# Differential attention: scores moved between the first four and the last two transpositions of a step

## The chip, the cores and the metric

One core of a Trainium2 chip runs the whole program. The metric is device time in microseconds (us), the median of several executions. The kernel before takes 3136.89 us (three runs, 3135.58 to 3138.68).

## What is computed

The program is a two-layer block (LRU, convolution, forgetting attention, gated feed-forward) followed by two hybrid layers. The change touches one part of each hybrid layer, differential attention over 512 latent tokens (and, in the first hybrid layer, 256 context tokens). For each of four heads there are two sets of scores, and the output uses the difference of their softmaxes:

```python
def diff_attn_dense(q, k, v, lam):
    s = jnp.einsum('bqhcd,bkhcd->bhcqk', q, k).astype(jnp.float32) * (q.shape[-1] ** -0.5)
    p = jax.nn.softmax(s, axis=-1)
    a = (p[:, :, 0] - lam * p[:, :, 1]).astype(v.dtype)
    return jnp.einsum('bhqk,bkhv->bqhv', a, v)
```

The result is normalised per head (`diff_head_norm`) and multiplied by a gate.

## The kernel before

The program is one instruction list per engine, written by hand: TensorE (PE), VectorE (DVE), ScalarE (ACT), GpSimd (POOL) and SyncE (SP). Each engine takes its own list strictly in the order written, and semaphores hold it where another engine's result is needed.

Differential attention is a list of jobs, one for a head and 128 query tokens: in hybrid layer 0 five jobs for each head (four latent ones with 768 keys, then one context job that covers all 256 context queries with 256 keys), 20 in all; in hybrid layer 1 four latent jobs for each head, 16 in all. One job n passes through these pieces:

- **scores** (PE, L970; matmuls L986, for context L977): two sets, into PSUM banks 0 to 2 for even n and 3 to 5 for odd n. It waits until the exponentials of job n-2 have freed these banks.
- **maxima** (DVE, L2393, instruction L2398): negative row maxima of both sets, straight from PSUM.
- **exps** (ACT, L1674, instruction L1680): two exponentials of 768 elements (four of 256 for a context job), with their sums; the last frees the score banks.
- **probs** (DVE, L2401; L2407, L2410, L2416): reciprocals, and the difference of the two sets. It waits for the freed banks.
- **transposes** (PE, L992): four 128x128 transpositions into bank 6 (L1001), which wait for probs; then, for a latent job, two more into the first half of bank 7 (L1006). Bank 7 is also where values writes its result, so these two wait for evac of job n-1.
- **evac on ACT** (L1685): copies bank 6 (L1689) and then bank 7 (L1693) to the buffer DAT.
- **values** (PE, L1009, L1020): six matmuls of 128 columns with V (four for a context job), into bank 7. It waits for both copies by ACT.
- **evac on DVE** (L2419, L2424): scales the result out of bank 7. **squares** (ACT, L1695) sums its squares.
- After the last latent job and after the context job of a head: **scale** (DVE, L2433), **turn** (PE, L1024, L1029), which transposes the scaled head back through bank 6, and **post** (DVE, L2438).

The order of the work is that of the step loops. In step n, PE issues scores(n+2), values(n-1), transposes(n) and, where job n-2 ended a head, turn(n-2). ACT issues exps(n+1), evac(n), squares(n-1). DVE issues probs(n), post(n-3), maxima(n+2), evac(n-1), scale(n-2). After the last job PE goes on with the first products of the next stage, `pe_head` (L579, matmuls L594 to L596).

Of the kernel before, what the change touches and what calls it, by code (L numbers as in the profile page):

```python
# [249 lines left out]
def build(nc, x, ctx_in, w8, wb, wm, wf_in, wg_in, params, rows, lru_w, sgu_w, sgu_b, rope, rot, nbias, vlat, mrow, wrow,  # L250
# [9 lines left out]
    def sem(name):  # L260
        if name not in sems:
            sems[name] = cx.enter_context(nc.semaphore(name))
        return sems[name]
# [154 lines left out]
    DE, DAT0, DSQ = cv(2, 2 * TA), cv(TA), cv(P)  # L418
    assert cv.at <= hyb_at + 2 * KT * SLAB
    DAT = [DAT0, RST[:, 0:TA]]  # L420
# [52 lines left out]
    def past(name, layer):  # L473

        return in_layer0[name] if layer else 0
# [26 lines left out]
    def wait(eng, s, v):  # L502

        if not (isinstance(v, int) and v <= 0):
            eng.wait_ge(s, v)
# [460 lines left out]
    def pe_da(pe, st):  # L966
        ly, jobs = st.layer, st.jobs
        nj = len(jobs)

        def scores(j):  # L970
            n, h, p = j["n"], j["h"], 3 * (j["n"] % 2)
            wait_free(pe, st, p, n // 2)
            lo, hi = slice(0, 64), slice(64, 128)
            if j["ctx"]:
                for qb in range(2):
                    for c, r in ((0, lo), (1, hi)):
                        mm = pe.matmul(PS[:, p + c, qb * TC:(qb + 1) * TC], Q[r, h, T + qb * P:T + (qb + 1) * P],  # L977
                                       K[r, h, T:TA], start=True, stop=True, skip_group_check=True)
            else:
                q0 = P * j["qb"]  # L980
                half = sem("da_half")
                for i, (r, b, c0, k0, k1) in enumerate(((lo, p + 1, 0, T, TA), (hi, p + 2, 0, TC, TA),
                                                        (lo, p, 0, 0, T), (hi, p + 1, TC, 0, TC))):
                    if i == 3:
                        pe.wait_ge(half, past("da_half", ly) + sum(not k["ctx"] for k in jobs[:n]) + 1)
                    mm = pe.matmul(PS[:, b, c0:c0 + k1 - k0], Q[r, h, q0:q0 + P], K[r, h, k0:k1], start=True,  # L986
                                   stop=True, skip_group_check=True)
                    if i == 0:
                        mm.then_inc(half, 1)
            mm.then_inc(full[p], 1)  # L990

        def transposes(j):  # L992
            n = j["n"]
            pe.wait_ge(sem("da_probs"), past("da_probs", ly) + n + 1)
            wait_free(pe, st, 6, n)
            outs = sum(i["last"] for i in jobs[:max(n - 2, 0)])
            wait(pe, sem("da_y"), past("da_y", ly) + outs)
            e = DE[:, n % 2, :]
            for i in range(4):
                o = i if not j["ctx"] else 2 * (i % 2) + i // 2  # L1000
                mm = pe.transpose(PS[:, 6, o * P:(o + 1) * P], e[:, i * P:(i + 1) * P], IDENT[:, :])  # L1001
            mm.then_inc(full[6], 1)
            wait(pe, sem("da_evac"), past("da_evac", ly) + n)
            if not j["ctx"]:
                for i in range(4, 6):
                    mm = pe.transpose(PS[:, 7, (i - 4) * P:(i - 3) * P], e[:, i * P:(i + 1) * P], IDENT[:, :])  # L1006
                mm.then_inc(full[7], 1)

        def values(j):  # L1009
            n, h = j["n"], j["h"]  # L1010
            nl = sum(not i["ctx"] for i in jobs[:n + 1])
            pe.wait_ge(freed[6], st["free", 6] + n + 1)
            pe.wait_ge(freed[7], st["free", 7] + nl)
            wait(pe, sem("da_evac"), past("da_evac", ly) + n)
            at = DAT[n % 2]
            for qb in range(1 + j["ctx"]):
                tiles = (4, 5) if j["ctx"] else range(6)
                for i, t in enumerate(tiles):
                    o = i * TC + qb * P if j["ctx"] else i * P
                    mm = pe.matmul(PS[:, 7, qb * P:(qb + 1) * P], at[:, o:o + P], V[:, t, h * P:(h + 1) * P],  # L1020
                                   start=i == 0, stop=i == len(tiles) - 1, skip_group_check=True)
            mm.then_inc(sem("da_o"), 1)

        def turn(j):  # L1024

            pe.wait_ge(sem("da_scaled"), past("da_scaled", ly) + j["g"] + 1)
            pe.wait_ge(freed[6], st["free", 6] + min(j["n"] + 3, nj))
            for i in range(2 if j["ctx"] else 4):
                mm = pe.transpose(PS[:, 6, i * P:(i + 1) * P], DO[:, j["g"] % 2, i * P:(i + 1) * P], IDENT[:, :])  # L1029
            mm.then_inc(sem("da_turned"), 1)  # L1030

        pe.wait_ge(sem("rope_done"), past("rope_done", ly) + 8)
        for b in range(8):
            wait_free(pe, st, b, 0)
        scores(jobs[0])
        scores(jobs[1])
        for n in range(nj + 2):
            if n + 2 < nj:
                scores(jobs[n + 2])
            if 0 <= n - 1 < nj:  # L1040
                values(jobs[n - 1])
            if n < nj:
                transposes(jobs[n])
            else:
                pe_head(pe, st.merge, n - nj)
            if 0 <= n - 2 < nj and jobs[n - 2]["last"]:
                turn(jobs[n - 2])
        if st.merge.ctx:
            pe_head(pe, st.merge, 2)
# [620 lines left out]
    def act_da(act, own, st):  # L1670
        ly, jobs = st.layer, st.jobs
        nj = len(jobs)

        def exps(j):  # L1674
            n, p = j["n"], 3 * (j["n"] % 2)
            act.wait_ge(sem("da_max"), past("da_max", ly) + n + 1)
            k, w = (4, TC) if j["ctx"] else (2, TA)
            src = PS[:, p:p + 3, :].rearrange("p a b -> p (a b)")
            for i in range(k):
                ins = act.activation(DE[:, n % 2, i * w:(i + 1) * w], src[:, i * w:(i + 1) * w], ACT.Exp,  # L1680
                                     bias=SMALL[:, 4 * (n % 2) + i:4 * (n % 2) + i + 1],
                                     accum_out=SMALL[:, 16 + 4 * (n % 4) + i:17 + 4 * (n % 4) + i])
            ins.then_inc(freed[p], 1)

        def evac(j):  # L1685
            n = j["n"]
            at = DAT[n % 2]
            act.wait_ge(full[6], st["full", 6] + n + 1)
            act.activation(at[:, 0:T], PS[:, 6, :], ACT.Copy).then_inc(freed[6], 1)  # L1689
            if not j["ctx"]:  # L1690
                nl = sum(not i["ctx"] for i in jobs[:n])
                act.wait_ge(full[7], st["full", 7] + nl + 1)
                act.activation(at[:, T:TA], PS[:, 7, 0:TC], ACT.Copy).then_inc(freed[7], 1)  # L1693

        def squares(j):  # L1695
            n, g = j["n"], j["g"]
            act.wait_ge(sem("da_evac"), past("da_evac", ly) + n + 1)
            for i in range(2) if j["ctx"] else (j["qb"],):
                c = 40 + 4 * (g % 2) + i
                own.wait()  # L1700
                own.mark(act.activation(DSQ[:, :], DO[:, g % 2, i * P:(i + 1) * P], ACT.Square,
                                        accum_out=SMALL[:, c:c + 1]))
            if j["last"]:
                k = 2 if j["ctx"] else 4
                ss, rs = (SMALL[:, c + 4 * (g % 2):c + 4 * (g % 2) + k] for c in (40, 48))
                own.wait()
                own.link(act.activation(rs, ss, ACT.Ln, bias=EPSC[:, 0:1], scale=1.0 / P))
                act.activation(rs, rs, ACT.Exp, scale=-0.5).then_inc(sem("da_rs"), 1)

        act.preload_act_table_set("natural_log_exp_and_others")  # L1710
        for part in range(2):
            act_head(act, st.merge, part)
        exps(jobs[0])
        for n in range(nj + 1):
            if n + 1 < nj:
                exps(jobs[n + 1])
            if n < nj:
                evac(jobs[n])
            if 0 <= n - 1 < nj:
                squares(jobs[n - 1])  # L1720

# [663 lines left out]
    def dve_da(dve, own, st):  # L2385
# [60 lines left out]
        for n in range(nj + 3):  # L2446
            if n < nj:
                probs(jobs[n])
            if 0 <= n - 3 < nj and jobs[n - 3]["last"]:
                post(jobs[n - 3])  # L2450
            if n + 2 < nj:
                maxima(jobs[n + 2])
            if 0 <= n - 1 < nj:
                evac(jobs[n - 1])
            if 0 <= n - 2 < nj and jobs[n - 2]["last"]:
                scale(jobs[n - 2])

# [689 lines left out]
```

## Time and profile before

| | |
|---|---|
| median of three runs | 3136.89 us |
| the profiled execution's own time | 3136.75 us |
| its span in the profile | 3135.0 us |
| PE busy | 96% of the span |
| DVE, ACT busy | 47%, 37% |
| differential attention, hybrid layer 0 (first transposition to the first product of the next stage) | 79.07 us |
| the same, hybrid layer 1 | 65.49 us |

A busy PE is not PE at its peak, since the ends of matmuls are modelled. What one piece costs is therefore read as the distance from its start to the start of the next piece on the same engine. An engine's idle time before an instruction stands in square brackets, with what ended it.

### The profile page before, as it was taken

What the parts mean: (1) busy time and instruction counts of PE and PEld (TensorE: products, weight loads), DVE (VectorE), ACT (ScalarE), POOL (GpSimd) and SP (SyncE); (2) the same over time, 40 slices, a digit from 0 to 9 for tenths busy, and PEclk for the clock granted to TensorE, in tenths of its full rate; (3) what the DMA queues carried; (4) which work ended last, traced back from release to release, by engine and by line L of the source; (5) the groups of instructions that cost most, each with busy time, mean ns of one, the idle gap of its engine ahead of it and who ended that gap; (6) DMA issues with size and microseconds to landing.
All of it is one profiled execution on the core that took longest, in us unless ns stands there. A gap on an engine that the chain in (4) does not pass through costs nothing.

```text
span 3135.0 us, 38597 instructions
## 1 busy us (share of the span) xinstructions
PE 3008.1 (96%) x15614; PEld 2446.7 (78%) x15614; DVE 1479.8 (47%) x1976; ACT 1155.7 (37%) x1828; POOL 148.9 (5%) x206
## 2 busy tenths in 40 slices
PE   7999999999999998989999899999999999999998
PEld 5777888777778887867888788868877778878776
DVE  4645454545454556176252532163444635352344
ACT  4335233425352444145243431163222534241342
POOL 1000000110000000000000400100000000200100
PEclk9999999999999999999999999999999999999999
DMA  4242232331322221110111311211111022221322
GB/s 176 94 148 104 111 108 100 125 125 50 121 94 94 95 96 57 68 34 28 50 55 61 91 65 52 96 58 48 53 68 67 14 77 75 101 95 54 115 71 81
DMA packets 44460, 256.81 MB, mean 82 GB/s; under 512 B 6344, under 2 KB 6352, under 8 KB 20512
## 3 DMA queue, kind: packets, MB, share of 16 engines
q1 hardware_dynamic: 30528, 204.30, 18.3%
q0 software_dynamic: 13792, 50.51, 4.9%
q8 instruction: 104, 1.70, 0.2%
q14 instruction: 36, 0.29, 0.0%
HBM read 250.51 MB, written 4.28 MB: 81 GB/s over the span
## 4 chain that ended last, share of the span: by engine, by line
PE 86%; DVE 8%; ACT 3%; DMA 2%; issue 1%; POOL 1%; DVEq 0%; SPq 0%; ACTq 0%; POOLq 0%
PE PS L805 13%; PE PS L806 13%; PE PS L807 13%; PE PS L786 7%; PE PS L785 7%; PE PS L787 7%; PE PS L751 2%; PE PS L750 2%; PE PS L749 2%; DVE SMALL L2398 2%; PE PS L986 1%; DMA W<-in_w 1%; PE PS L1100 1%; PE PS L1084 1%; PE PS L1074 1%
## 5 line engine op out<-in xcount | busy, mean ns | idle before, releaser
L805 PE MATMUL PS<-HHX,WHX 128*128 128x512 f32 (+1 forms) x1456 | 510.5, 351 | 8.7 <-DVE WLX L2248 6.4
L806 PE MATMUL PS<-HL,WHX 128*128 128x512 f32 (+1 forms) x1456 | 511.5, 351 | 0.0
L1565 ACT ACTIVATE WHX<-W 128x2048 fp32r<-128x2048 f32 (+1 forms) x102 | 174.6, 1712 | 578.6 <-DMA W<-in_w 390.5
L807 PE MATMUL PS<-HHX,WLX 128*128 128x512 f32 (+1 forms) x1024 | 356.5, 348 | 0.0
L2248 DVE TENSOR_TENSOR WLX<-W,WHX 128x2048 fp32r<-128x2048 f32 x60 | 137.5, 2292 | 381.8 <-ACT WHX L1565 381.8
L805 PEld LDWEIGHTS PS<-HHX,WHX 128*128 128x128 f32 x1456 | 278.2, 191 | 47.0 <-DVE WLX L2248 7.3
L806 PEld LDWEIGHTS PS<-HL,WHX 128*128 128x128 f32 x1456 | 277.0, 190 | 36.6
L786 PE MATMUL PS<-HL,WH 128*128 128x512 f32 x672 | 265.4, 395 | 0.0
L785 PE MATMUL PS<-HH,WH 128*128 128x512 f32 x672 | 263.3, 392 | 0.0
L787 PE MATMUL PS<-HH,WL 128*128 128x512 f32 x672 | 261.7, 389 | 0.0
L2248 DVE TENSOR_TENSOR WL<-W,WH 128x2048 fp32r<-128x2048 f32 x68 | 155.9, 2292 | 221.8 <-ACT WH L1565 221.8
L1565 ACT ACTIVATE WH<-W 128x2048 fp32r<-128x2048 f32 x68 | 130.3, 1915 | 282.6 <-PE PS L787 252.1
L807 PEld LDWEIGHTS PS<-HHX,WLX 128*128 128x128 f32 x1024 | 195.6, 191 | 24.4
L2286 DVE SCALAR_TENSOR_TENSOR ARENA<-PS,PC,ARENA 128x511 f32<-128x511 f32 (+1 forms) x176 | 131.6, 748 | 73.1 <-ACT ARENA L1593 60.0
L2248 DVE TENSOR_TENSOR WLM<-W,WHX 128x1024 fp32r<-128x1024 f32 (+1 forms) x42 | 70.6, 1680 | 179.5 <-ACT WHX L1565 179.4
L807 PE MATMUL PS<-HHX,WLM 128*128 128x512 f32 (+1 forms) x432 | 154.9, 359 | 0.0
L785 PEld LDWEIGHTS PS<-HH,WH 128*128 128x128 f32 x672 | 125.8, 187 | 30.8
L787 PEld LDWEIGHTS PS<-HH,WL 128*128 128x128 f32 x672 | 126.1, 188 | 28.2
L786 PEld LDWEIGHTS PS<-HL,WH 128*128 128x128 f32 x672 | 126.2, 188 | 27.2
L749 PE MATMUL PS<-WHX,HHX 128*128 128x512 f32 x288 | 119.6, 415 | 0.0
L751 PE MATMUL PS<-WHX,HL 128*128 128x512 f32 x288 | 112.7, 391 | 0.0
L750 PE MATMUL PS<-WLX,HHX 128*128 128x512 f32 x288 | 112.5, 391 | 0.0
(532 smaller groups left out, 5938.2 us busy)
## 6 DMA issues: line engine op xcount, KB each, us to landing
W<-in_w SPq DMA_DIRECT2D x172, 1024.0 KB, 4.7
XC<-in_wm POOLq DMA_DIRECT2D x12, 1024.0 KB, 5.0
H<-in_wm POOLq DMA_DIRECT2D x12, 1024.0 KB, 5.6
W<-in_wb SPq DMA_DIRECT2D x24, 512.0 KB, 3.4
W<-in_w SPq DMA_DIRECT2D x8, 768.0 KB, 4.0
ARENA<-mrow POOLq DMA_DIRECT2D x12, 256.0 KB, 4.3
ARENA<-wrow POOLq DMA_DIRECT2D x12, 256.0 KB, 4.7
PR<-in_nbias POOLq DMA_DIRECT2D x12, 256.0 KB, 2.9
```

The source lines that it names most:

```text
L749: pe.matmul(PS[:, t, :], xh, wh[:, s, c], start=s == 0 and k == 0, stop=False)
L750: pe.matmul(PS[:, t, :], xh, wl[:, s, c], start=False, stop=False)
L751: mm = pe.matmul(PS[:, t, :], xl, wh[:, s, c], start=False, stop=s == 1 and k == 3)
L785: pe.matmul(PS[:, b, :], WH[:, s, c], hi(k), start=k == 0, stop=False)
L786: pe.matmul(PS[:, b, :], WH[:, s, c], lo(k), start=False, stop=False)
L787: mm = pe.matmul(PS[:, b, :], WL[:, s, c], hi(k), start=False, stop=k == kb - 1)
L805: pe.matmul(dst, wh[:, s, c], hi[:, k, t0:t1], start=k == 0, stop=False)
L806: pe.matmul(dst, wh[:, s, c], lo[:, k, t0:t1], start=False, stop=False)
L807: mm = pe.matmul(dst, wl[:, s, c], hi[:, k, t0:t1], start=False, stop=k == kb - 1)
L1565: act.activation(dst[:, s, 0:n], W[:, s, 0:n], ACT.Copy).then_inc(wh_ready[s], 1)
L2248: dve.tensor_tensor(lo[:, s, 0:n], W[:, s, 0:n], hi[:, s, 0:n].bitcast(F32), ALU.subtract).then_inc(wl_ready[s], 1)
L2286: ins = dve.scalar_tensor_tensor(out=CB[:, m, d:T], in0=PS[:, m, 0:T - d], scalar=PC[:, bass.ds(i * 16 + (base + 4 * m + 2 - d), 1)], in1= ...
```

## The change

Three lists are written in another order. On PE, scores(n+2) leaves its place at the head of step n and goes between the first four and the last two transpositions of the same step. On ACT, the two exponentials of job n+1 are put apart: one ahead of the copy of bank 6, one ahead of the copy of bank 7. On DVE, evac(n-1) is put ahead of maxima(n+2). No instruction is added or removed, and no size changes.

```diff
@@ pe_da
                 mm = pe.transpose(PS[:, 6, o * P:(o + 1) * P], e[:, i * P:(i + 1) * P], IDENT[:, :])
             mm.then_inc(full[6], 1)
+
+        def late_transposes(j):
+            n = j["n"]
+            e = DE[:, n % 2, :]
             wait(pe, sem("da_evac"), past("da_evac", ly) + n)
             if not j["ctx"]:
                 for i in range(4, 6):
@@
         for n in range(nj + 2):
-            if n + 2 < nj:
-                scores(jobs[n + 2])
             if 0 <= n - 1 < nj:
                 values(jobs[n - 1])
             if n < nj:
                 transposes(jobs[n])
+                if n + 2 < nj:
+                    scores(jobs[n + 2])
+                late_transposes(jobs[n])
             else:
                 pe_head(pe, st.merge, n - nj)
@@ act_da
-        def exps(j):
+        def exps(j, half):
...
-            for i in range(k):
+            for i in range(k // 2 * half, k // 2 * (half + 1)):
...
-            ins.then_inc(freed[p], 1)
+            if half:
+                ins.then_inc(freed[p], 1)
...
-        exps(jobs[0])
+        for half in range(2):
+            exps(jobs[0], half)
         for n in range(nj + 1):
             if n + 1 < nj:
-                exps(jobs[n + 1])
+                exps(jobs[n + 1], 0)
             if n < nj:
                 evac(jobs[n])
+            if n + 1 < nj:
+                exps(jobs[n + 1], 1)
+            if n < nj:
+                late_evac(jobs[n])
@@ dve_da
+            if 0 <= n - 1 < nj:
+                evac(jobs[n - 1])
             if n + 2 < nj:
                 maxima(jobs[n + 2])
-            if 0 <= n - 1 < nj:
-                evac(jobs[n - 1])
```

On PE, a stretch of hybrid layer 0: before, the scores of job 5 (L986), the values of job 2 (L1020), the four and the two transpositions of job 3 (L1001, L1006), and the scores of job 6.

```order
L986 MATMUL PS<-ARENA 128x256
L986 MATMUL PS<-ARENA 128x512 x2
L986 MATMUL PS<-ARENA 128x256
L1020 MATMUL PS<-ARENA 128x128 x6
L1001 MATMUL PS<-IDENT,ARENA 128x128 x4
L1006 MATMUL PS<-IDENT,ARENA 128x128 x2
L986 MATMUL PS<-ARENA 128x256
```

Now the same pieces, from the values of job 2 to the values of job 3 (values is L1024 here, the last two transpositions L1010).

```order
L1024 MATMUL PS<-ARENA 128x128 x6
L1001 MATMUL PS<-IDENT,ARENA 128x128 x4
L986 MATMUL PS<-ARENA 128x256
L986 MATMUL PS<-ARENA 128x512 x2
L986 MATMUL PS<-ARENA 128x256
L1010 MATMUL PS<-IDENT,ARENA 128x128 x2
L1024 MATMUL PS<-ARENA,RST 128x128 x6
```

The scores of job 5 have moved behind the four transpositions of job 3, and the last two transpositions now stand directly ahead of the values of the same job.

On DVE, the same steps before: the end of probs(2) (L2416), maxima(4) (L2398), evac(1) (L2424), probs(3) (L2407, L2410, L2416), maxima(5), evac(2).

```order
L2416 SCALAR_TENSOR_TENSOR ARENA<-ARENA,SMALL 128x768
L2398 TENSOR_REDUCE SMALL<-PS 128x4
L2424 TENSOR_SCALAR PR<-PS,SMALL 128x128
L2407 RECIPROCAL SMALL<-SMALL 128x2
L2410 SCALAR_TENSOR_TENSOR SMALL<-SMALL,LAM 128x1
L2416 SCALAR_TENSOR_TENSOR ARENA<-ARENA,SMALL 128x768
L2398 TENSOR_REDUCE SMALL<-PS 128x2
```

And now (L2431, L2439, L2413, L2422, L2425 are the former L2416, L2424, L2398, L2407, L2410).

```order
L2431 SCALAR_TENSOR_TENSOR ARENA<-ARENA,SMALL 128x768
L2439 TENSOR_SCALAR PR<-PS,SMALL 128x128
L2413 TENSOR_REDUCE SMALL<-PS 128x4
L2422 RECIPROCAL SMALL<-SMALL 128x2
L2425 SCALAR_TENSOR_TENSOR SMALL<-SMALL,LAM 128x1
L2431 SCALAR_TENSOR_TENSOR ARENA<-ARENA,SMALL 128x768
L2439 TENSOR_SCALAR PR<-PS,SMALL 128x128
```

The evacuation stands ahead of the maxima; in both orders the maxima of job n+2 stand ahead of the probs of job n+1.

## Rows read from the trace of the kernel before

**Rows 1.** The page: busy us, share of the span and instructions of each engine.
```profile
PE 3008.1 (96%) x15614; PEld 2446.7 (78%) x15614; DVE 1479.8 (47%) x1976; ACT 1155.7 (37%) x1828; POOL 148.9 (5%) x206
```

**Rows 2.** Windows, both stages: length, busy PE, PEld, DVE, ACT, POOL; PEclk; DMA.
```profile
1378.69:1457.76 79.07, 71.59 (x491) 55.69 (x491) 66.50 (x117) 59.62 (x182) 0.00 (x0) 1.00 0.03 13
2431.22:2496.71 65.49, 61.63 (x405) 48.26 (x405) 52.04 (x80) 45.65 (x124) 0.00 (x0) 0.96 0.04 16
```

**Rows 3.** Timeline, a latent step of layer 1: start us, us, engine, line, [idle before].
```profile
2442.17 1.56 PE L986 MATMUL PS<-ARENA 64*128 64x256 f32 x8
...
2443.66 1.60 PE L1020 MATMUL PS<-ARENA 128*128 128x128 f32 x12
...
2443.78 1.76 DVE L2398 TENSOR_REDUCE SMALL<-PS 128x2 f32<-128x1536 f32 x1 [0.65 <-PE PS L986]
...
2445.11 0.60 PE L1001 MATMUL PS<-IDENT,ARENA 128*128 128x128 f32 x4
2445.46 0.34 DVE L2424 TENSOR_SCALAR PR<-PS,SMALL 128x128 f32<-128x128 f32 x1
2445.72 0.15 DVE L2407 RECIPROCAL SMALL<-SMALL 128x2 f32<-128x2 f32 x1
2445.74 0.60 ACT L1689 ACTIVATE RST<-PS 128x512 f32<-128x512 f32 x1 [1.02 <-PE PS L1001]
...
2445.85 0.44 PE L1006 MATMUL PS<-IDENT,ARENA 128*128 128x128 f32 x2
...
2446.16 1.02 DVE L2416 SCALAR_TENSOR_TENSOR ARENA<-ARENA,SMALL 128x768 f32<-128x768 f32 x1
...
2446.22 1.56 PE L986 MATMUL PS<-ARENA 64*128 64x256 f32 x8
```

**Rows 4.** Timeline, layer 0's first step: probs, first transpositions, maxima followed by probs.
```profile
1377.62 1.02 DVE L2416 SCALAR_TENSOR_TENSOR ARENA<-ARENA,SMALL 128x768 f32<-128x768 f32 x1
1378.55 1.75 DVE L2398 TENSOR_REDUCE SMALL<-PS 128x2 f32<-128x1536 f32 x1
...
1378.69 0.66 PE L1001 MATMUL PS<-IDENT,ARENA 128*128 128x128 f32 x4 [1.85 <-DVE ARENA L2416]
...
1380.22 0.15 DVE L2407 RECIPROCAL SMALL<-SMALL 128x2 f32<-128x2 f32 x1
```

**Rows 5.** Timeline: scale and turn ahead of scores (layer 0), turn ahead of values (layer 1).
```profile
1399.05 0.68 DVE L2433 TENSOR_TENSOR PR<-PR,SMALL 128x512 f32<-128x512 f32 x1
...
1399.78 0.66 PE L1029 MATMUL PS<-IDENT,PR 128*128 128x128 f32 x4 [0.16 <-DVE PR L2433]
...
1400.37 1.56 PE L986 MATMUL PS<-ARENA 64*128 64x256 f32 x8
...
2488.61 0.63 PE L1029 MATMUL PS<-IDENT,PR 128*128 128x128 f32 x4 [0.19 <-DVE PR L2433]
2489.08 1.50 PE L1020 MATMUL PS<-ARENA,RST 128*128 128x128 f32 x12
```

**Rows 6.** Timeline: a context job's scores and maxima.
```profile
1384.03 1.14 PE L977 MATMUL PS<-ARENA 64*128 64x256 f32 x8
...
1385.21 1.23 DVE L2398 TENSOR_REDUCE SMALL<-PS 128x4 f32<-128x1024 f32 x1 [0.23 <-PE PS L977]
```

**Rows 7.** Timeline, layer 0's end: last two transpositions directly ahead of values.
```profile
1450.11 0.44 PE L1006 MATMUL PS<-IDENT,ARENA 128*128 128x128 f32 x2
1451.11 1.58 PE L1020 MATMUL PS<-ARENA,RST 128*128 128x128 f32 x12 [0.56 <-ACT RST L1689]
```

**Rows 8.** Timeline, layer 1's start, under a lower clock: scores and their maxima.
```profile
2432.69 2.93 PE L986 MATMUL PS<-ARENA 64*128 64x256 f32 x8
...
2435.67 1.76 DVE L2398 TENSOR_REDUCE SMALL<-PS 128x2 f32<-128x1536 f32 x1 [1.46 <-PE PS L986]
```

**Rows 9.** Windows: the end of forgetting attention, an earlier stage (columns as in rows 2).
```profile
785.00:790.00 5.00, 3.89 (x35) 3.65 (x35) 0.97 (x3) 1.24 (x2) 0.00 (x0) 1.00 0.00 0
790.00:795.00 5.00, 4.54 (x17) 3.76 (x17) 1.68 (x3) 0.63 (x1) 0.00 (x0) 0.66 0.00 0
```

More of the change, by code:

```diff
@@ L1689, in evac, with late_evac @@
             act.activation(at[:, 0:T], PS[:, 6, :], ACT.Copy).then_inc(freed[6], 1)
+        def late_evac(j):
+            n = j["n"]
+            at = DAT[n % 2]
             if not j["ctx"]:
```

## The prediction, made before the changed kernel ran

> **What bounds the kernel now.** I read the page first, for the share of each engine: PE is busy 96% of the span [rows 1], so PE's list is the bound almost everywhere. Then the windows around the two stages that the change touches: 79.07 and 65.49 us, PE busy 91% and 94% in them, DVE 84% and 79% [rows 2]. Together they are 4.6% of the span, so nothing here can move the time by more than that in the good direction, and DVE is nearly as loaded as PE. Then the timeline of one latent step in layer 1 [rows 3], where the reader should measure from start to start on one engine. PE: scores to values 2443.66 - 2442.17 = 1.49, values to first transpositions 1.45, these to the last two 0.74, those to the next scores 0.37; the step is 4.05 us (2442.17 to 2446.22). The 0.74 holds a wait: the last two transpositions (2445.85) begin just after DVE's evacuation (2445.46, 0.34 long). Four transpositions with something ready behind them take 0.59 (1399.78 to 1400.37) [rows 5], so the wait is 0.15, and PE's own work is 3.90 of the 4.05. DVE's maxima wait for PE's scores, 0.65 us idle [rows 3]; DVE has slack, and it has it because scores(n+2) is issued at the head of step n, a whole step ahead of the probs that follow its maxima in DVE's list.
>
> **What the change takes away.** The wait of 0.15 goes: the scores now cover the evacuation. That is worth 0.15 on most of some 30 latent steps, about 4 us, if PE stays the bound.
>
> **What it adds on PE.** The last two transpositions now stand directly ahead of the values of the same job, which need ACT's copy of bank 7. Until now 1.49 us of scores lay between. The end of layer 0 has this order already: transpositions at 1450.11, values at 1451.11 with 0.56 idle, waiting for ACT [rows 7]. So 1.00 stands for 0.37. PE's step would be 1.45 + 0.59 + 1.49 + 1.00 = 4.53, if nothing else held it.
>
> **What it adds across engines.** This is the larger term. On DVE maxima(n+2) still stands ahead of probs(n+1). On PE scores(n+2) now stands behind the first transpositions of job n, which wait for probs(n). So the chain is: first transpositions(n), scores(n+2), maxima(n+2), probs(n+1), first transpositions(n+1), and it closes once per step; before, it closed once in two steps. Its length:
> - transpositions to scores: 0.59 [rows 5]
> - scores to maxima: 2443.78 - 2442.17 = 1.61 [rows 3]
> - maxima to the reciprocal directly behind it: 1380.22 - 1378.55 = 1.67 [rows 4]
> - reciprocal to the difference: 2446.16 - 2445.72 = 0.44 [rows 3]
> - difference to first transpositions: 1378.69 - 1377.62 = 1.07 [rows 4]
>
> The sum is 5.38 us. It is more than PE's 4.53, so the step becomes 5.38 for 4.05, and the 0.15 saved and the 0.63 added on PE both disappear in slack. ACT does not lengthen it: its first half of exps(n+1) follows maxima(n+1), the copy of bank 6 starts 0.63 after the transpositions (2445.74 for 2445.11) [rows 3], and the second half is through some two us after them, while probs(n+1) starts only 0.59 + 1.61 + 1.67 = 3.87 after. The evacuation on DVE falls into DVE's new wait for scores and costs nothing.
>
> **Steps of another length**, measured from first transpositions to first transpositions:
> - The scores and maxima issued are a context job's: scores to maxima 1.18, maxima 1.23 long for 1.76 [rows 6], so 1.15 for 1.67. 0.59 + 1.18 + 1.15 + 0.44 + 1.07 = 4.43. A context job's probs I take at the latent price.
> - A turn of a latent head (three in each layer; the fourth is behind the last step). Turn waits for scale, which stands behind maxima: 3.87 after the transpositions. Scale to turn 0.73 (1399.05 to 1399.78), turn to values 0.47 (2488.61 to 2489.08) [rows 5], values to transpositions 1.45: 6.52. Here PE, not DVE, comes last. PE waits some 2.1 us in it, between the last two transpositions (done about 2.5 us in) and the turn (4.6).
> - A context job's turn (three, in layer 0) has half the transpositions: 0.47 becomes about 0.25, 6.30.
> - The step before the last has no scores: copy of bank 6 at 0.63, 0.5 to the next ACT instruction, 1.0 for the second half of the exponentials (estimates, from the copy's 0.60 and the 1.02 that DVE takes over the same 768 elements [rows 3]), 0.5 for the copy of bank 7, 1.45 for values: 4.05.
> - The first step: probs(0) is where it was, but scores(2) no longer fills PE's wait for it. PE is then idle for the 1.85 that it waits now [rows 4], the 1.56 of the scores that went, and what it waited ahead of them. Layer 1's first steps already ran at half of the clock (0.96 over the stage) [rows 2]: there scores to maxima take 2435.67 - 2432.69 = 2.98 [rows 8] for 1.61. I take this for the first step of both layers, with 0.3 more for the transpositions: 5.38 + 1.37 + 0.3 = 7.05.
>
> **The sum.** Layer 0 has 19 intervals from job 0 to job 19: one of 7.05, seven of 5.38, four of 4.43, three of 6.52, three of 6.30, one of 4.05, together 104.9. Then the tail, from the last job's first transpositions to the next stage's product, in which the order is the old one: 0.63 and 0.60 for the copy [rows 3], 0.1 to values, 8 of the 12 PE instructions of a latent values, 0.9: 2.2. So 107.1 for 79.07 [rows 2], +28. Layer 1 has 15 intervals: 7.05, ten of 5.38, three of 6.52, 4.05, together 84.5, and for the tail of a latent job 0.59, 1.00 [rows 7] and 1.35, 2.9: 87.4 for 65.49 [rows 2], +22. Together +50. Everything behind a stage starts that much later and nothing absorbs it, since PE runs the next products without a gap. The clock may fall at some of the six places where turns hold PE; one fall costs up to 1.67 (the 1.37 + 0.3 above), and I count about one, +2. Against the execution's own time, 3136.75 + 50 + 2 = 3188.75, so 3189; this execution lies 0.14 below the median of the runs, which does not matter.
>
> **Bounds.** The order added is not in the trace, so from both sides: the least that the step can be is PE's own work without the new wait, 3.90 (a gain of 4 to 5 us in all); PE's list with its new wait gives 4.53; the chain gives 5.38; the chain at half clock gives 5.38 + 1.67 = 7.05. I take 5.38, since every link of it stands in rows at full clock, and each is a true dependence.
>
> **Rivals.**
> - *PE stays the bound.* If the maxima did not sit between (their start hidden by work issued ahead), a step would be 4.53: +0.48 on about 29 steps, +14 us, 3151. For it: PE is busy 91 to 94% [rows 2]. Against it: DVE's list has maxima(n+2) ahead of probs(n+1), and 5.38 is larger than 4.53 by 0.85, far more than reading errors.
> - *A gain, no loss.* The mechanism is the removed 0.15 with ACT's copy of bank 7 early enough. Its place is the last two transpositions; it gives 3136.75 - 5, about 3132. It decides only if the chain is below 3.90 and the copy costs PE nothing, and both are contradicted by rows [rows 3, 4, 7].
> - *The clock falls again and again.* The new step leaves PE idle about 1.3 of 5.38 us, and 2.1 at once at the turns. At the end of forgetting attention PE was busy 3.89 of 5.00 us (78%) with the clock at 1.00, and in the next 5 us it was 0.66 [rows 9], so a share like the new one does not exclude a fall from 2.4 to 1.2 GHz. If half of the 33 steps ran at half clock: 33 x 0.5 x 1.67 = 28 more, 3217; if all, 3245. Against it: the falls in rows are short, and the steps have work in all of their parts. The Trainium skill, page "TensorE: Matmul & The Clock Gate", section "A second HAM failure mode: psum-queue depth-cycling", says that frequent small idle gaps between groups of matmuls make the clock swing between its two levels. By that rule this rival would be the result; in layer 0 PE had 7.5 us of small gaps in 79.07 and the clock stayed at 1.00 [rows 2], so the trace does not bear it out for gaps of that share; the new share is larger.
>
> **How the numbers follow.** A measurement of this kernel can tell about 0.2%, 6.3 us, from no change. The chain: 0.78, 3189, its own range 3182 (no fall at all, and the first steps at full clock) to 3199 (a fall at each of the six turn places, +10). The falling clock throughout: 0.12, 3217. PE as the bound: 0.07, 3151. Gain or nothing: 0.03, 3132. From 3177 to 3212 the chain is held almost whole, with a part of the clock case, a little over 8 in 10. Faster by over 0.2%: 0.02, within 0.2%: 0.01, slower: 0.97.
>
> **What the profile after should show.** The first four transpositions start 5.3 to 5.4 us apart in plain latent steps, each ended by a wait for DVE's difference (about 0.8 us idle); maxima begin 2.2 us after them with some two us of DVE idle in front; the reciprocal comes directly behind the maxima. Values wait about 0.56 for ACT. Turns sit behind 2 us of PE idle. The two stages last about 107 and 87 us, and the stages around them are unchanged. The forecast is wrong if the spacing is near 4.5 (PE bound) or near 7 in many steps (clock), or if maxima start before the first transpositions of their step.

## The result, and the profile after

| | before | after |
|---|---|---|
| median | 3137.78 us (4 runs) | 3197.11 us (4 runs, 3194.51 to 3203.78) |
| ratio | | 1.0193, 95% interval 1.0177 to 1.0209 |
| span of the profiled execution | 3135.0 us | 3192.9 us |
| differential attention, layer 0 | 79.07 us | 114.22 us |
| the same, layer 1 | 65.49 us | 89.47 us |

The change makes the kernel 59 us slower. The forecast was 3189, its range 3177 to 3212. The two stages are 35.15 and 23.98 us longer, 59.1 together; the stretch between them is 972.63 us for 973.46, the one behind them 637.18 for 638.29, so nothing else moved by more than 1.2 us. About 2 us of layer 1's 65.49 before is a low clock in its first step (5.93 us; it is 3.7 us in three other runs that keep PE's list of before in the stages), so the 23.98 is that much too small for the change itself.

The page after, its line of busy times, which answers to [rows 1]:

```profile
PE 3022.7 (95%) x15614; PEld 2458.8 (77%) x15614; DVE 1480.9 (46%) x1976; ACT 1159.6 (36%) x1828; POOL 146.6 (5%) x206
```

The instruction counts are the same and the busy times nearly so: the loss is waiting. The windows of the two stages (columns as in [rows 2]: length, busy time of PE, PEld, DVE, ACT, POOL with instruction counts, then the granted clock):

```profile
1379.40:1493.62 114.22, 84.64 (x498) 64.37 (x499) 66.94 (x117) 62.46 (x184) 0.00 (x0) 0.90 0.02 9
2466.25:2555.72 89.47, 66.66 (x413) 50.97 (x413) 52.43 (x80) 48.41 (x126) 0.00 (x0) 0.96 0.03 12
```

PE is busy 74% in both, for 91% and 94% before. In layer 0 the granted clock fell from 1.00 to 0.90.

The timeline of a plain latent step in layer 1 after, the counterpart of [rows 3]. Read it as the chain: first transpositions (L1001), scores (L986), maxima (L2413), reciprocal (L2422), difference (L2431); the row at the top is the difference that releases these transpositions.

```profile
2477.79 1.02 DVE L2431 SCALAR_TENSOR_TENSOR ARENA<-ARENA,SMALL 128x768 f32<-128x768 f32 x1
...
2478.72 0.35 DVE L2439 TENSOR_SCALAR PR<-PS,SMALL 128x128 f32<-128x128 f32 x1
2478.86 0.66 PE L1001 MATMUL PS<-IDENT,ARENA 128*128 128x128 f32 x4 [0.78 <-DVE ARENA L2431]
2479.45 1.56 PE L986 MATMUL PS<-ARENA 64*128 64x256 f32 x8
2479.55 0.60 ACT L1695 ACTIVATE ARENA<-PS 128x512 f32<-128x512 f32 x1 [1.10 <-PE PS L1001]
...
2480.94 0.44 PE L1010 MATMUL PS<-IDENT,ARENA 128*128 128x128 f32 x2
2481.05 1.76 DVE L2413 TENSOR_REDUCE SMALL<-PS 128x2 f32<-128x1536 f32 x1 [1.99 <-PE PS L986]
2481.41 0.38 ACT L1703 ACTIVATE ARENA<-PS 128x256 f32<-128x256 f32 x1 [0.38 <-PE PS L1010]
...
2481.89 1.58 PE L1024 MATMUL PS<-ARENA 128*128 128x128 f32 x12 [0.52 <-issue]
2482.73 0.15 DVE L2422 RECIPROCAL SMALL<-SMALL 128x2 f32<-128x2 f32 x1
...
2483.18 1.02 DVE L2431 SCALAR_TENSOR_TENSOR ARENA<-ARENA,SMALL 128x768 f32<-128x768 f32 x1
```

0.59 + 1.60 + 1.68 + 0.45, and 1.07 from the difference to the transpositions that it releases, are 5.39 us; the forecast had 5.38. PE waits for DVE (0.78) and DVE waits for PE (1.99) in the same step: each is idle while the other works, which is how a closed chain looks in a timeline. The evacuation (L2439) ends before the last two transpositions ask for it. Values (L1024) idle 0.52 us; the profile names no releaser, but ACT's copy of bank 7 (L1703, to 2481.79), on which values depend, ends 0.10 us ahead of them.

The timeline around a turn in layer 0, for the part that the forecast took too small (L1033 is the turn, L2448 scale):

```profile
1437.84 0.66 PE L1001 MATMUL PS<-IDENT,ARENA 128*128 128x128 f32 x4 [2.15 <-DVE ARENA L2431]
1438.43 1.56 PE L986 MATMUL PS<-ARENA 64*128 64x256 f32 x8
...
1442.44 0.66 PE L1033 MATMUL PS<-IDENT,PR 128*128 128x128 f32 x4 [2.09 <-DVE PR L2448]
...
1442.94 2.43 PE L1024 MATMUL PS<-ARENA 128*128 128x128 f32 x12
...
1445.16 1.06 PE L1001 MATMUL PS<-IDENT,ARENA 128*128 128x128 f32 x4
```

PE idles 2.15 and 2.09 us within some 7 us, and then values take 2.43 for 1.58 and transpositions 1.06 for 0.66: the clock has gone to its lower level behind the second wait. At the other two such places of layer 0 it had fallen already behind the 2.15, ahead of the turn:

```profile
1408.46 0.66 PE L1001 MATMUL PS<-IDENT,ARENA 128*128 128x128 f32 x4 [2.15 <-DVE ARENA L2431]
1409.05 2.84 PE L986 MATMUL PS<-ARENA 64*128 64x256 f32 x8
...
1467.21 1.12 PE L1001 MATMUL PS<-IDENT,ARENA 128*128 128x128 f32 x4 [2.15 <-DVE ARENA L2431]
1468.26 2.71 PE L986 MATMUL PS<-ARENA 64*128 64x256 f32 x8
```

Scores take 2.84 and 2.71 us there for 1.56, and the turns follow after waits of 1.84 and 2.09 us. The spacing of first transpositions over layer 0 is 7.86, 5.99, 4.43, 5.39, 5.39, 8.02, 6.18, 4.40, 5.39, 5.39, 7.32, 6.88, 4.39, 5.40, 5.38, 9.17, 6.63, 4.40, 3.99 us. Most of the excess lies at the turns (8.02, 7.32, 9.17, forecast 6.52) and at the steps behind the last two of them (6.88 and 6.63, forecast 6.30); the first two steps (7.86 and 5.99, forecast 7.05 and 5.38) carry 1.4 us. In layer 1 one turn of three is long too (7.72; the others 6.74).

### The profile page after: what moved, and what is told of

Same layout as the page of the kernel before. It is cut to its first block, busy times and chain, and to the rows that moved or that the text cites. A ratio compares the mean times of both kernels' runs of the same rounds, so it can differ in the third digit from the quotient of the medians.

```text
span 3192.9 us, 38597 instructions
## 1 busy us (share of the span) xinstructions
PE 3022.7 (95%) x15614; PEld 2458.8 (77%) x15614; DVE 1480.9 (46%) x1976; ACT 1159.6 (36%) x1828; POOL 146.6 (5%) x206
## 4 chain that ended last, share of the span: by engine, by line
PE 86%; DVE 9%; ACT 2%; issue 1%; DMA 1%; POOL 1%; DVEq 0%; SPq 0%; ACTq 0%; POOLq 0%
PE PS L805 13%; PE PS L806 13%; PE PS L807 13%; PE PS L786 7%; PE PS L785 7%; PE PS L787 7%; PE PS L751 2%; PE PS L750 2%; PE PS L749 2%; DVE SMALL L2413 2%; PE PS L986 2%; PE PS L1105 1%; PE PS L1089 1%; PE PS L1079 1%; PE PS L1074 1%
```

## Experiments

Each ran beside the kernel before on the same chip, with the before median of its batch in brackets. "Stages" are layer 0 and layer 1, first transposition to the next stage's first product, from the profile (before: 79.07 and 65.49).

**One part alone.** `pe_da` of the change, with `act_da` and `dve_da` of before:

```diff
+                if n + 2 < nj:          # pe_da only
+                    scores(jobs[n + 2])
+                late_transposes(jobs[n])
```

> Only PE's list is the changed one; ACT and DVE keep the lists of before. Theory (loops closed by the order of the lists): DVE's evacuation of job n-1 again stands behind maxima(n+2), so the last two transpositions wait for it, values for ACT's copy behind them, and the next first transpositions for values. Loop: 0.59 + 1.61 + 1.67 + 0.39 (evacuation to last two) + 1.00 + 1.45 = 6.71 us a latent step, 2.66 more than before; about 28 such steps: +75 us, near 3213, with more from clock falls. Rival (the three parts each cost on their own and add up to the +59): at most +59, below 3197. Rival (PE's own list with one new wait, 4.53 a step): +14, near 3152.

Measured 3238.1 us [3138.38], ratio 1.0323 (1.0306 to 1.0341); stages 132.78 and 110.78, together 99.0 more than before. DVE and the last two transpositions in a step of layer 1:

```profile
2519.29 1.76 DVE L2403 TENSOR_REDUCE SMALL<-PS 128x2 f32<-128x1536 f32 x1 [4.71 <-PE PS L986]
2520.96 0.34 DVE L2429 TENSOR_SCALAR PR<-PS,SMALL 128x128 f32<-128x128 f32 x1
...
2521.36 0.44 PE L1010 MATMUL PS<-IDENT,ARENA 128*128 128x128 f32 x2 [2.12 <-DVE PR L2429]
```

The evacuation behind the maxima holds the last two transpositions 2.12 us, and undisturbed steps are 6.58 us (6.71 expected). The granted clock is 0.85 in both stages, which goes with the rest of the +99 over the +75; that rest was not taken apart further. Both rivals fall: the parts do not add up, the DVE part of the change wins back 41 of what the PE part costs.

This run also shows how little the length of a wait says on the clock. The first window holds three plain steps of layer 1, the second a plain step that follows a little later; in each of the four steps PE waits the same 2.12 and 0.52 us:

```profile
2538.24:2557.99 19.75, 11.83 (x81) 9.15 (x80) 9.98 (x15) 8.51 (x23) 0.00 (x0) 1.00 0.00 1
2578.12:2586.24 8.12, 5.48 (x29) 4.42 (x28) 3.33 (x5) 4.08 (x12) 0.00 (x0) 0.75 0.01 2
```

The clock stayed at 1.00 in the three and fell to 0.75 in the fourth, in which values took 2.90 us for 1.58.

`act_da` of the change alone:

```diff
+                exps(jobs[n + 1], 0)    # act_da only
             if n < nj:
                 evac(jobs[n])
+            if n + 1 < nj:
+                exps(jobs[n + 1], 1)
```

> Only ACT's list is the changed one. Theory: the second half of exps(n+1) now stands behind the copy of bank 6, which waits for the first transpositions of job n, and scores(n+3) at the head of PE's next step waits for it. Loop: 0.63 + 0.5 + 1.05 + 1.49 (scores) + 1.45 (values) = 5.1 us a latent step, +31 us, near 3169. Rival (ACT has slack, its split costs nothing here): within 3 us of before.

Measured 3172.59 us [3138.38], ratio 1.0114 (1.0096 to 1.0132); plain latent steps 5.10 us, stages 97.17 and 82.21. Under the order of before, scores wait for the split exponentials:

```profile
2485.37 1.56 PE L986 MATMUL PS<-ARENA 64*128 64x256 f32 x8 [0.58 <-ACT ARENA L1680]
```

So ACT has slack in the sum of its work, not in the order of it.

`dve_da` of the change alone:

```diff
+            if 0 <= n - 1 < nj:         # dve_da only
+                evac(jobs[n - 1])
             if n + 2 < nj:
                 maxima(jobs[n + 2])
```

> Only DVE's list is the changed one: evacuation ahead of maxima. Theory: plain latent steps lose the wait of 0.15 (3.90 for 4.05), but steps around a turn get longer, since maxima and scale wait for the evacuation, which waits for values: by the same working +7 us in layer 0 and +3 in layer 1, near 3148. Rival (the evacuation ahead is a pure gain of the wait): -4 us, near 3134.

Measured 3153.63 us [3138.38], ratio 1.0056 (1.0036 to 1.0076). Plain latent steps are 3.91 us for 4.05, as expected, but a turn now waits 1.83 us for scale, which stands behind the late maxima:

```profile
2488.36 0.66 PE L1029 MATMUL PS<-IDENT,PR 128*128 128x128 f32 x4 [1.83 <-DVE PR L2433]
```

Steps with a latent head's turn take 7.90, 6.30 and 9.26 us in layer 0 for 5.57, and 8.00, 6.39 and 5.63 in layer 1 for 4.87. The stages are 93.18 and 69.27 us, so +14.1 and +3.8 for the +7 and +3 expected; layer 0 is the part that was put too low, and its granted clock was 0.91.

`pe_da` and `dve_da` of the change, `act_da` of before:

> PE's and DVE's lists are the changed ones, ACT keeps the list of before. Theory: the loop of 5.38 us (first transpositions, scores, maxima, probs) has no piece of ACT in it, so the time is that of the full change within 3 us, 3194 to 3200. Rival (ACT's split, which costs time by itself, carries part of the +59): clearly less, 3165 to 3185.

Measured 3196.9 us [3138.38], ratio 1.0194 (1.0177 to 1.0211); plain steps 5.39 us, stages 113.27 and 88.56. It is the time of the full change. ACT's split, +34 by itself, costs nothing here: it lies beside the longer chain of PE and DVE.

**The crossing itself.** As the last one, with the scores one place earlier, ahead of the four transpositions:

```diff
             if n < nj:
-                transposes(jobs[n])
                 if n + 2 < nj:
                     scores(jobs[n + 2])
+                transposes(jobs[n])
                 late_transposes(jobs[n])
```

> PE and DVE as in the full change and ACT as before, but on PE the scores stand one place earlier: values, scores, four transpositions, last two. The same pieces of PE with the same stall of 1.00 between the last two transpositions and values. Theory: the scores no longer stand behind the transpositions that wait for probs, so the loop of one step opens; what is left is PE's own 1.45 + 1.49 + 0.59 + 1.00 = 4.5 to 4.6 us a latent step: +21 us against before, near 3159, or 3165 with clock falls. Rival (the loss lies in the stall of values behind the last two transpositions): no better than the 3197 with both parts.

Measured 3160.01 us [3138.34], ratio 1.0075 (1.0058 to 1.0092); stages 91.61 and 75.45, clock 0.98. One swap of neighbours gives back 37 us. Maxima now start 0.1 us behind the first transpositions instead of 2.2:

```profile
2455.46 0.66 PE L1001 MATMUL PS<-IDENT,ARENA 128*128 128x128 f32 x4
2455.57 1.76 DVE L2403 TENSOR_REDUCE SMALL<-PS 128x2 f32<-128x1536 f32 x1 [1.15 <-PE PS L986]
...
2457.12 1.58 PE L1024 MATMUL PS<-ARENA 128*128 128x128 f32 x12 [0.79 <-ACT ARENA L1694]
```

The step is 4.66 us (4.5 to 4.6 expected): PE's own pieces and the stall of values, which is left, 1.17 us from the last two transpositions to values for the 1.00 of the working.

**A known delay in two places.** The full change with a DVE copy of 256 elements in each step, behind the maxima or ahead of them:

```diff
+        def pad():
+            dve.tensor_copy(RST[:, TA:TA + 256], RST[:, TA:TA + 256])
...
                 maxima(jobs[n + 2])
+                pad()
```

> The full change, and a DVE copy of 256 elements that nobody needs behind each maxima of the steps (18 in layer 0, 14 in layer 1). Theory: it stands in the loop, so each step grows by all of its length, some 0.3 us by estimate: 32 x 0.3 = +10 us against the full change, near 3207. Rival (PE or the clock, not DVE's order, sets the step): no change, 3197.

> The same copies ahead of the maxima. Theory: they fall in DVE's wait for scores, about two us long in each step, and cost nothing: within 3 us of the full change, 3194 to 3200. Rival (DVE's busy time as such costs): the same as with the copies behind, near 3207.

The copy stands in the chain like this:

```profile
2482.53 1.76 DVE L2416 TENSOR_REDUCE SMALL<-PS 128x2 f32<-128x1536 f32 x1 [1.99 <-PE PS L986]
2484.20 0.28 DVE L2409 COPY RST<-RST 128x256 f32<-128x256 f32 x1
2484.40 0.16 DVE L2425 RECIPROCAL SMALL<-SMALL 128x2 f32<-128x2 f32 x1
```

It takes 0.20 us start to start (I had put 0.3), and plain steps behind it are 5.59 us for 5.39: all of its length. Ahead of the maxima they stay 5.39. These step lengths are what the test shows. The medians are 3207.89 and 3202.42 us [3138.34], ratios 1.0230 (1.0213 to 1.0247) and 1.0199 (1.0182 to 1.0216). That the first comes near the 3207 expected is in part luck: 32 x 0.20 is 6.4 us of the +10.8 over the full change, not all of it, and the granted clock is lower in both stages (0.88 and 0.94 for 0.90 and 0.96). The second lies outside the 3194 to 3200 expected. In its profiled execution the first transposition of layer 0 comes at 1385.62 us for 1379.40, before any changed instruction, its four runs lie between 3196.35 and 3205.10, and layer 0's stage is 2.7 us longer at a granted clock of 0.87 for 0.90 (layer 1's is 0.2 shorter). So the whole time is a poor witness here and the step lengths are the evidence. In a plain step DVE's busy time as such costs nothing; its place in the chain does.

**The clock.** The full change with matmuls that nobody needs in PE's long waits (36 ahead of a stage's first transpositions, 12 ahead of each turn, 12 behind a context job's values):

```diff
+        def fill(k):
+            for _ in range(k):
+                pe.matmul(PS[:, 6, 0:128], IDENT[:, :], IDENT[:, :], start=True, stop=True, skip_group_check=True)
```

> The full change, and matmuls nobody needs in PE's three long waits: 36 ahead of the first transpositions of a layer, 12 ahead of each turn, 12 behind the values of a context job (128x128, into bank 6 while it is free). Theory: the 9 us that the stages took beyond the working (59.1 measured for 50) and the clock part of it are falls to half clock behind these waits; with PE kept at work the clock stays at 1.00 and the time falls by 8 to 12 us, to about 3187. Rival (the excess is in waits, not in the clock): no change, or slower by what the fillings delay, 3197 to 3201.

Measured 3196.55 us [3138.34], ratio 1.0183 (1.0166 to 1.0200). The windows are the stage of layer 0, the stretch to layer 1's stage, that stage, and the rest:

```profile
1381.89:1489.66 107.77, 95.78 (x716) 81.00 (x715) 66.88 (x117) 62.47 (x184) 0.00 (x0) 1.00 0.01 4
1489.66:2467.41 977.75, 950.15 (x5444) 805.55 (x5442) 386.98 (x572) 300.65 (x519) 58.92 (x82) 0.99 0.19 64
2467.41:2553.79 86.38, 70.09 (x486) 56.23 (x485) 52.43 (x80) 48.41 (x126) 0.00 (x0) 1.00 0.01 4
2553.79:3195.10 641.31, 609.37 (x3099) 494.03 (x3097) 267.04 (x373) 221.32 (x359) 48.45 (x64) 0.98 0.24 82
```

Inside the stages the theory holds: clock 1.00, and 9.5 us less (107.77 and 86.38 for 114.22 and 89.47). But the time is that of the plain change and not the 3187 expected. A part of what eats the gain is the fillings themselves: the 36 matmuls ahead of a stage's first transpositions stand outside the stage windows, and they last longer than the wait they fill. Ahead of layer 1:

```profile
2464.14 1.02 DVE L2441 SCALAR_TENSOR_TENSOR ARENA<-ARENA,SMALL 128x768 f32<-128x768 f32 x1
...
2467.41 0.60 PE L1001 MATMUL PS<-IDENT,ARENA 128*128 128x128 f32 x4
```

From the difference to the first transpositions it is 3.27 us for the 1.07 of the plain change, 2.20 us lost, and the same 3.27 (1378.62 to 1381.89) stands ahead of layer 0. So of the 5.1 us by which the stretch between the stages is longer (977.75 for 972.63) 2.2 are the filling, and 2.9 are not explained; the stretch behind layer 1, which holds no filling, is 4.1 us longer (641.31 for 637.18). These remainders are small: in the ten profiled executions without fillings whose stretches can be set beside these, the stretch between the stages is 972.6 to 974.8 us and the one behind 636.2 to 639.0, so the filled kernel is 0.8 and 2.3 us above the longest.

To see whether more PE instructions do that wherever they stand, the kernel before got 100 such matmuls at the head of PE's list:

```diff
         pe.wait_ge(consts, 8)
+        for _ in range(100):
+            pe.matmul(PS[:, 3, 0:128], IDENT[:, :], IDENT[:, :], start=True, stop=True, skip_group_check=True)
```

> The kernel before with 100 matmuls nobody needs at the very start of PE's list, where PE waits 13 us for its first input; nothing else. Open is why the filled full change, whose two stages became 9.5 us shorter, took 4 to 5 us more between the stages and 4 behind them. Theory A (200 more PE instructions ahead shift where instructions are loaded, and the loads cost time everywhere behind): the stretches between and behind the stages longer than 973.5 and 638.3 us, 3141 to 3150. Theory B (that cost is tied to fillings within the stages): both stretches as before, 3136 to 3140.

Measured 3153.82 us [3137.45], ratio 1.0049 (1.0032 to 1.0066). They took 24.9 us and so were not hidden: layer 0's stage begins at 1393.21, 14.5 us later, which puts the time above both ranges. The rest leans to theory A, no more: 975.82 us between the stages and 639.7 behind them are 2.4 and 1.4 more than before, but only 1.1 and 0.7 above the longest of the ten executions without fillings. The page's count of instruction packets went from 104 to 105 here and to 107 in the filled change. That the loading of instructions is the cause is a guess; it stays open.

**Towards a better kernel.** Only `dve_da` of before is touched: scale and evacuation ahead of the maxima.

```diff
+            if 0 <= n - 2 < nj and jobs[n - 2]["last"]:
+                scale(jobs[n - 2])
+            if 0 <= n - 1 < nj:
+                evac(jobs[n - 1])
             if n + 2 < nj:
                 maxima(jobs[n + 2])
```

> PE's and ACT's lists as before; only on DVE scale(n-2) and evac(n-1) stand ahead of maxima(n+2). Theory: no loop closes early, since the scores stay at the head of PE's step; the wait of 0.15 before the last two transpositions goes, and scale, now ahead of maxima and evacuation, no longer makes the turn late (which is what cost the DVE part alone its time at the turns). By the working 2 us less in layer 0 and 1 in layer 1: 3135, or -0.1%. Rival (maxima held up by the evacuation's wait for values cost as in the DVE part alone): +10 to +15, 3150.

> The same, and matmuls nobody needs in PE's waits at the start of each stage (14 behind the first two scores, 10 behind the third). Theory: layer 1's first step, 5.93 long for 3.74 in layer 0 since the clock had fallen, becomes 3.74: another -2 us, 3133. Rival (matmuls put into PE's list cost time outside the stages, as 4 to 5 us in each stretch of the filled full change): no gain over the run without them, or slower.

> The kernel before with the same fillings at the start of the two stages alone. Theory: layer 1's first step 3.74 for 5.93, -2 us, 3136. Rival (fillings cost outside): 3138 to 3142, with the stretches between and behind the stages longer than 973.5 and 638.3 us.

Medians 3136.92, 3134.47 and 3137.05 us [3137.57]; ratios 1.0000 (0.9990 to 1.0010), 0.9990 (0.9981 to 0.9998) and 0.9998 (0.9989 to 1.0006). The stages of the first are:

```profile
1380.22:1457.79 77.57, 71.81 (x491) 55.90 (x491) 66.01 (x118) 60.12 (x182) 0.00 (x0) 1.00 0.03 14
2431.33:2494.30 62.97, 59.44 (x404) 46.92 (x405) 51.59 (x80) 45.66 (x124) 0.00 (x0) 1.00 0.04 16
```

In layer 0 that is 1.5 us less than before, with plain latent steps of 3.91 and turns of 4.93 for 5.57; in layer 1 2.5 less, of which 2.2 is a first step of 3.74 for 5.93 that the clock gave without a filling. The kernel with 100 matmuls at its head and the one with DVE's part alone have 3.73 there, also without a filling at that place, so the long first step seems to belong to the single execution. Two or three microseconds are at the edge of what such runs can tell. With the fillings the stages are 77.51 and 62.91, and the time is 0.1% below before with an interval that just excludes 1. The fillings alone show nothing in the time; layer 1's first step is 3.68 in their profile, which proves nothing for them, since it is 3.7 without them too. There is no version here that beats the kernel before by a margin worth having.

## Why the prediction was right, and where a size was off

- **The chain closes once per step: shown.** 5.39 us for 5.38, link by link in the timeline. Delay in the chain counts in full (0.20 for 0.20), the same delay outside it not at all, and moving the scores ahead of the transpositions opens the chain (4.66).
- **The evacuation and ACT's work are hidden: shown.** The full change and the one without ACT's split take the same time.
- **PE's own new stall: shown as slack.** 0.52 us of idle before values, as forecast near 0.56, not on the path until the chain is opened, where it grows to 0.79.
- **Steps of another kind.** Context scores 4.39 to 4.43 for 4.43; the step before the last 3.99 and 4.25 for 4.05; first steps 7.86 and 7.22 for 7.05. The 1.67 added to a first step was the clock, as forecast: with PE kept at work the first steps are 5.34 and 5.33. A latent turn at full clock is 6.74 for 6.52: values to transpositions takes 1.65 us there for 1.45, since these transpositions write bank 6 and wait until post (DVE) has read the turned head out of it.
- **The sum.** 107.1 and 87.4 were forecast at full clock, the first steps apart. With the clock held, the filled kernel has 107.77 and 86.38. That they lie so close is in part luck: with first steps of 5.38 in place of 7.05 the forecast for full clock is 105.4 and 85.7, and the filled stages are 2.3 and 0.7 longer, at the turns (6.76 and 6.81 for 6.52), at the steps behind them in layer 0 (6.53 for 6.30) and at the three steps there with a filling behind a context job's values (5.75 for 5.38). Two figures of the working are a little off: six falls of 1.67 in place of none give 3197 for the upper end of the chain's own range and not 3199, since 3189 already holds one, and no fall with full-clock first steps gives 3183 and not 3182; the 3245 of the third rival comes to 3244.
- **The term that was mis-sized is the falls of the clock:** "I count about one, +2". The stages took 59.1 us more for the 50 of the sum. Of these 9 us some 6.4 stand at the falls: all three turn places of layer 0 and one of layer 1 fell, and the steps behind two of the turns ran partly at the lower level; that is the term put at 2. Another 1.6 are in the first two steps of layer 0 and the first of layer 1, at a granted clock of 0.50, 0.88 and 0.69, and 1.3 are the 0.22 of each of the six turns, which is not the clock. Against the 3194.72 of the profiled execution the forecast is 6 us low (7 in the stages, less 1.2 in the other stretches); the median of the runs lies another 2.4 us higher. The working had the 2.1 us of idle in the turn step but not the other 2.15 us just ahead of it in layer 0, behind which two of that layer's three falls came. That wait follows a context job, whose step has no last two transpositions and short values.
- **The Trainium skill's** "TensorE: Matmul & The Clock Gate", section "A second HAM failure mode: psum-queue depth-cycling", that small idle gaps between groups make the clock swing, is not borne out for small gaps: steps with 0.78 and 0.52 us of idle stayed at 1.00 (21.56 us in a row in layer 1). Behind the first steps the falls came at waits of about 2 us, and in the run of PE's part alone a wait of 2.12 us in every plain step went with both 1.00 and 0.75.

## What to carry to other kernels

Before moving an instruction past another engine's wait, write down the chain through all lists and count how many steps it spans: work issued two ahead is only two ahead if it is issued before the step's own wait. The busy sums (DVE 84% before, 59% after) say nothing on this. And a reordering has to be judged as a set: DVE's part costs 15 us alone and saves 41 beside PE's.

## What was not expected of the hardware

- TensorE left 2.4 GHz for 1.2 GHz behind waits of about 2 us: in layer 0 behind a wait of 2.15 us at two places (scores 2.84 and 2.71 us for 1.56) and behind the 2.09 of a turn at the third (values 2.43 us for 1.58), in layer 1 behind the 2.09 of one turn of three. Such a wait does not always do it: with PE's part alone, steps with a wait of 2.12 us each stayed at 1.00 three in a row, and the same step fell later to 0.75. What decides is open. Filling the waits with matmuls kept the granted clock at 1.00.
- Those fillings went with stretches hundreds of microseconds away that are 2.9 us (their own overrun of 2.2 taken off) and 4.1 us longer than after the plain change, at a granted clock of 0.99 and 0.98 in both kernels. That is 0.8 and 2.3 us above the longest of the ten executions without fillings, and it rests on one profiled execution of each kernel. The cause is open.
